# Both MLP products of a 1024-wide block as seven block products, in units of 1024 inner channels

## The reference

```python
h = rms_norm(x, g_mlp[l])
f = jnp.square(jax.nn.relu(jnp.einsum("bsd,df->bsf", h, w_1[l])))   # 1024 -> 4096 inner channels
x = x + jnp.einsum("bsf,fd->bsd", f, w_2[l])                        # 4096 -> 1024
```

## Time and profile before

| what | value |
|---|---|
| median of 3 runs | 2386.34 us (2386.21 to 2386.46) |
| the profiled execution | 2386.64 us |
| its span | 2384.8 us |
| PE, DVE, ACT, POOL busy | 2369.0, 1549.4, 902.7, 84.4 us |
| granted TensorE clock, mean | 0.998 |
| moved by DMA | 138.43 MB, 58 GB/s |

### The profile page before, as it was taken

How to read it: one execution, slowest core, us unless ns; L and a number is a source line. 1 busy time by engine, 2 the same in 40 slices (tenths; PEclk the granted TensorE clock), 3 DMA queues, 4 the chain that set the end, 5 groups by cost and what they waited for, 6 DMA issues and landing times.

```text
span 2384.8 us, 26302 instructions
## 1 busy us (share of the span) xinstructions
PE 2369.0 (99%) x10688; PEld 1923.4 (81%) x10688; DVE 1549.4 (65%) x2162; ACT 902.7 (38%) x1370; POOL 84.4 (4%) x103
## 2 busy tenths in 40 slices
PE   9999999999999999999999999999999999999998
PEld 7778688687788888888888888888888877888887
DVE  8899599598779744466655665534667544462377
ACT  6552442443512632333433343332343232222364
POOL 0000000000000000011111111000000000000000
PEclk9999999999999999999999999999999999999999
DMA  4201112012031112312212211112211111211222
GB/s 139 58 23 54 62 36 76 27 45 76 29 104 45 45 45 72 96 49 62 58 32 62 62 47 42 58 45 73 81 45 48 45 45 45 52 51 49 71 87 82
DMA packets 228321, 138.43 MB, mean 58 GB/s; under 512 B 15968, under 2 KB 219104, under 8 KB 228200
## 3 DMA queue, kind: packets, MB, share of 16 engines
q1 hardware_dynamic: 228200, 136.75, 19.5%
HBM read 127.78 MB, written 8.95 MB: 57 GB/s over the span
## 4 chain that ended last, share of the span: by engine, by line
PE 87%; DVE 8%; ACT 4%; issue 1%; DMA 0%; SPq 0%; DVEq 0%; ACTq 0%
PE bank L669 27%; PE bank L671 26%; PE bank L670 26%; PE bank L782 3%; DVE q_all L2872 1%; DVE v L2028 1%; PE bank L1055 1%; ACT whi L1193 1%; DVE uw L2638 0%; PE bank L1037 0%; PE bank L971 0%; DVE uc L2280 0%; DVE wlo L1899 0%; ACT un_hi L1209 0%; ACT bank L1419 0%
## 5 line engine op out<-in xcount | busy, mean ns | idle before, releaser
L669 PE MATMUL bank<-h_hi,whi 128*128 128x512 f32 x1984 | 780.2, 393 | 1.5 <-DVE h_lo L1921 1.1
L671 PE MATMUL bank<-h_hi,wlo 128*128 128x512 f32 x1984 | 773.0, 390 | 0.0
L670 PE MATMUL bank<-h_lo,whi 128*128 128x512 f32 x1984 | 772.6, 389 | 0.0
L669 PEld LDWEIGHTS bank<-h_hi,whi 128*128 128x128 f32 x1984 | 372.6, 188 | 83.0 <-DVE h_lo L1921 2.2
L670 PEld LDWEIGHTS bank<-h_lo,whi 128*128 128x128 f32 x1984 | 372.7, 188 | 79.5 <-issue 2.9
L671 PEld LDWEIGHTS bank<-h_hi,wlo 128*128 128x128 f32 x1984 | 372.7, 188 | 78.0
L1899 DVE TENSOR_TENSOR wlo<-raw,whi 128x1024 fp32r<-128x1024 f32 (+2 forms) x233 | 272.4, 1172 | 141.2 <-ACT whi L1193 139.6
L1193 ACT ACTIVATE whi<-raw 128x1024 fp32r<-128x1024 f32 (+2 forms) x233 | 232.5, 1004 | 269.0 <-PE bank L671 220.2
L2373 DVE SCALAR_TENSOR_TENSOR tmp<-bank,factor 128x512 f32<-128x512 f32 x64 | 44.2, 690 | 89.8 <-PE bank L671 89.8
L782 PE MATMUL bank<-v,gate_w 128*128 128x512 f32 x224 | 97.4, 592 | 0.0
L2392 DVE TENSOR_TENSOR x<-x,bank 128x512 f32<-128x512 f32 x96 | 65.7, 685 | 47.3 <-ACT bank L1500 46.4
(11 more groups left out here) (406 smaller groups left out, 3675.3 us busy)
## 6 DMA issues: line engine op xcount, KB each, us to landing
raw<-in_w_in SPq DMA_DIRECT2D x90, 512.0 KB, 3.7
raw<-in_w SPq DMA_DIRECT2D x40, 512.0 KB, 3.9
raw<-in_w_b_out SPq DMA_DIRECT2D x16, 384.0 KB, 3.1
raw<-in_w SPq DMA_DIRECT2D x24, 256.0 KB, 2.7
raw<-in_w SPq DMA_DIRECT2D x48, 128.0 KB, 2.2
raw<-in_w_out SPq DMA_DIRECT2D x11, 512.0 KB, 3.4
raw<-in_w_a_out SPq DMA_DIRECT2D x8, 512.0 KB, 3.8
raw<-in_w_o SPq DMA_DIRECT2D x8, 512.0 KB, 3.9
```

The source lines that it names most:

```text
L669: pe.matmul(target, lh, rh, start=start, stop=False, skip_group_check=True)
L670: pe.matmul(target, lh, rl, start=False, stop=False, skip_group_check=True)
L671: last = pe.matmul(target, ll, rh, start=False, stop=stop and point is not None, skip_group_check=True)
```

## The change

`PIECES`, `TURNS` and the plain first product go. The MLP becomes 28 **units** (`UNITS`), each of seven products. A unit covers two output tiles and 1024 input channels: four tiles are the first half of the blocks (a11, a12) and four the second (a21, a22). A product of a unit has 4 tiles x 3 = 12 matmuls. Units 0 to 15 (`UP`) are the first product, units 16 to 27 the second product of the first 3072 inner channels, in three sets of four (`DOWN`). Output tiles of the first product are u//4 * 8 + u % 4 and that plus 4.

- **Steps.** `ORDER` lists PE's steps, one product each: 1 and 5 of unit w, 7 of w-1, 2 of w, 3 of w-1, 6 of w, 4 of w-1. The PSUM scheme is the one of before.
- **Granules.** The left factor of each product is 128x512, a granule. ACT makes the high part (`ghi`), DVE the low part (`glo`), 4 or 5 steps ahead (`LEAD`); there are six rooms.
- **Weights.** SP loads two blocks of 128x1024 a unit, in two sets of buffers; `raw` is one of them. POOL forms the sums in place, as 128x512, four per unit.
- **Right sides.** Seven combinations of four tiles each (`c_hi`, `c_lo`) are kept. The first set is made from x in and after the output product, by scaled joins (L2510). For the sets of the second product they come from DRAM: b11 to t4 of units 0 to 11 are stored to `ff_dram`, 128x512 at a time, and loaded back in place of the set in use, four tiles of a name when its last product is done (`load_piece`, L635), and split 2 and 3 steps later (`pieces_at`).
- **Activation.** The results of a unit are emptied by DVE (`relu`, `relu_both`), squared by ACT, and their differences made by DVE (`three_differences`, `last_difference`).
- **The factor** is made from 8 one-column matmuls (`x1_stat`) and spread by 8 transposes.
- **The last 1024 inner channels** are units 12 to 15 of the first product; they are stored, and loaded as `ff_in` for the plain second product, whose first two column blocks PE computes together, tile by tile (`tiles_together`).

```diff
-PIECE = 4
-PIECES = 6
-TURNS = (0, 2, 1, 3)
+UP = D_FF // (2 * P)
+DOWN = FC - 1
+UNITS = UP + 4 * DOWN
+ORDER = [(w - late, n) for w in range(UNITS + 1) for n, late in ((1, 0), (5, 0), (7, 1), (2, 0), (3, 1), (6, 0), (4, 1))
+         if 0 <= w - late < UNITS]
+GRANULES = 6
+LEAD = (5, 5, 4, 4, 4, 5, 5)
...
+            def load_unit(u, *parts):
+                rows, row0, *columns = unit_columns(u)
+                for m in parts:
...
+                        for n in ((6, 3), (7, 4))[m]:
+                            w.wait_ge(*at("g", u - 2, n))
+                    sp.dma_start(unit_raw[u % 2][m][:].rearrange("p (k c) -> p k c", k=DT), tiles_of(rows, row0, DT, columns[m], P)).then_inc(
+                        *landed(f"unit{u % 2}_{m}", ("unit_in", u, m)))
...
+            for u in range(UNITS):
+                if 2 <= u + 1 < UNITS:
+                    load_unit(u + 1, 0)
+                store_ff(u - 2, "b21", "t4")
+                if u >= 2:
+                    load_piece(u - 2, "t4")
+                if 2 <= u + 1 < UNITS:
+                    load_unit(u + 1, 1)
+                load_piece(u, "b11")
+                load_piece(u, "t1")
...
+                store_ff(u - 1, "b22")
...
+                store_ff(u - 1, "b12", "t1", "t3", "t2")
+                load_piece(u, "t2")
...
-            def product(e, c, n):
+            def product(u, n):
...
+                room, name = granule_room(TURN[u, n]), RIGHT[n]
+                w.wait_ge(*at("g", u, n))
+                for p in range(HK):
+                    cs = slice(p * P, (p + 1) * P)
+                    w.wait_ge(*at("c_lo", unit_set(u), name, p))
+                    three_products(b[:], (ghi[room][:, cs], glo[room][:, cs]), (c_hi[name][p][:], c_lo[name][p][:]), n in (1, 5) and not p,
+                                   [("unit", u, n)] if p == HK - 1 else None)
...
+            for u, n in ORDER:
+                product(u, n)
+                if (u, n) == (0, 2):
+                    x1_stat()
+                if (u, n) == (0, 7):
+                    for half in range(2):
+                        w.wait_ge(*at("x1_r"))
+                        spread(0, half, "x1_factor", sum_banks[half])
...
-            for j in range(DT):
-                block(("w1", FC - 1, j, "end"), h2, "h2")
-            for j in range(DT - 2):
+            for half in range(2):
+                tiles_together([("w2", FC - 1, j) for j in range(2)], half, ff, f"ff{FC - 1}", order=FF_TILES)
+            for j in range(2, DT - 2):
...
+            for k, (u, n) in enumerate(ORDER):
+                granules(k + lead(k))
+                if n == 1:
+                    last_difference(u - 2)
...
+                if n == 6:
+                    three_differences(u - 1)
+                    third_seed(u)
...
+                new_combos(u, n)
...
+                pool.tensor_tensor(total[:], a21, a22, ALU.add).then_inc(*up("pool_done", ("sum", u, 5)))
+                w.wait_ge(*at("unit_in", u, 0))
+                pool.tensor_tensor(a21, a11, a21, ALU.subtract).then_inc(*up("pool_done", ("sum", u, 7)))
+                w.wait_ge(*at("g", u, 1))
+                w.wait_ge(*at("sum", u, 7))
+                pool.tensor_tensor(a11, total[:], a11, ALU.subtract).then_inc(*up("pool_done", ("sum", u, 6)))
+                w.wait_ge(*at("g", u, 2))
+                w.wait_ge(*at("sum", u, 6))
+                pool.tensor_tensor(a12, a12, a11, ALU.subtract).then_inc(*up("pool_done", ("sum", u, 3)))
```

More of the change, by code:

```diff
@@ L387, in build_program @@
[L387 to L391, removed]
+        ff_in = sb("ff_in", "h", 0, [P, DT, 2 * SEQ])
@@ L690, in hold @@
                 return banks[i]
-            def product(e, c, n):
-                kind, room, right = PRODUCTS[n]
-                k = number[kind, e, c]
+            def product(u, n):
                 if n == 1:
-                    b = hold(4 * (c % 2), "chain", e, c)
-                    hold(1, "first", e, c)
-                    w.wait_ge(*at("free", *earlier["chain", e, c]))
+                    b = hold(4 * (u % 2), "chain", u)
+                    hold(1, "first", u)
+                    w.wait_ge(*at("free", *earlier["chain", u]))
@@ L1542, in scalar, with first_seed @@
-            for j in range(DT):
-                ahead(number["w1", FC - 1, j, "end"] + 2)
-                for half in range(2):
-                    t = tmp[half]
-                    w.wait_ge(*at("relu", FC - 1, j, "end", half))
-                    act.activation(t[:], t[:], ACT.Square).then_inc(*did(("relu_square", FC - 1, j, "end", half)))
-                    w.wait_ge(*now("act_done"))
-                    w.wait_ge(*at("m", PIECES - 1, 3, 4))
-                    split_hi(("ff_hi", j, half), ff[0][j][:, cut(half)], t[:])
+            def first_seed(u):
+                w.wait_ge(*at("unit", u, 1))
+                w.wait_ge(*at("free", *earlier["first", u]))
+                act.activation(bank("first", u)[:], bank("chain", u)[:], ACT.Copy).then_inc(*did(("first_seed", u)))
@@ new lines, in fifth_copy, with fourth_seed @@
+            def fifth_copy(u):
+                w.wait_ge(*at("unit", u, 5))
+                if u >= 2:
+                    w.wait_ge(*at("fifth_used", u - 2))
+                act.activation(fifth[u % 2][:], bank("fifth", u)[:], ACT.Copy).then_inc(*did(("fifth_copy", u), ("free", "fifth", u)))
+            def fourth_seed(u):
+                w.wait_ge(*at("unit", u, 7))
+                w.wait_ge(*at("free", *earlier["fourth", u]))
+                act.activation(bank("fourth", u)[:], bank("chain", u)[:], ACT.Copy).then_inc(*did(("fourth_seed", u)))
@@ L1551, in scalar @@
+            for n in range(1, 4):
+                ff_part(n, 0)
+            for n in range(1, 4):
+                ff_part(n, 1)
             for j in range(DT - 2):
@@ new lines, in last_difference, with third_seed @@
+            def last_difference(u):
+                if not 0 <= u < WHOLE:
+                    return
+                w.wait_ge(*at("ff", u, "b21"))
+                w.wait_ge(*at("ff", u, "t2"))
+                difference(u, "t4", tmp[tmp_of(u, "b21")], tmp[tmp_of(u, "t2")])
+            def third_seed(u):
+                w.wait_ge(*at("unit", u, 6))
+                w.wait_ge(*at("fifth_copy", u))
+                w.wait_ge(*at("free", *earlier["third", u]))
+                dve.tensor_tensor(bank("third", u)[:], bank("chain", u)[:], fifth[u % 2][:], ALU.add).then_inc(*did(("third_seed", u)))
```

788 lines of the change are left out of this document (467 added, 321 removed).

## The result

The changed kernel takes 2352.61 us (2351.89 to 2353.5, 4 runs) where the kernel before takes 2386.4 (2386.21 to 2387.25): a ratio of 0.9858, 95% interval 0.9841 to 0.9875. The forecast was 2346.0, range 2341 to 2363. Faster was right, but by 33.8 us (1.4%), and the time is 6.6 us above the forecast. The seven-block products gave what was forecast; some 135 us behind them PE loses 8.4 us.

What follows compares the result with a forecast made beforehand. TensorE's matmul count times pitch was taken as the bound: 2386.3 - 43.5 + 0.9 = 2343.7 us, plus 1 (start), 0.5 (end) and 0.5 (set changes) gives 2345.7, forecast as 2346 us, range 2341 to 2363.

Steps and rivals of the forecast that it cites:

- 192 matmuls and the narrow ones: TensorE: 192 fewer matmuls at 0.2267 us save 43.5 us; one-column sums and small transposes, less the old sums, add 0.9.
- The start: From the output product's last matmul into unit 0: VectorE's joins and low parts nearly in time; 1 us of TensorE waiting.
- The set changes: Three changes of right sides: VectorE near 95% busy, 3 to 4 us behind at worst, without stopping TensorE; 0.5 us taken.
- the end: Start of the last plain second product: its tiles land and are split about when TensorE wants them; 0.5 us taken.
- GpSimd's addition: Four 128x512 additions per unit, taken at 1.48 us each, 5.9 us a unit, bounds 0.74 to 3.4 us each.
- The sharing: GpSimd's additions slow VectorE instructions reading two SBUF tensors: 0.45 us per us of GpSimd's work, 2.7 us a unit.
- by its numbers the exclusion is about half: Reading of the earlier trace: GpSimd and VectorE exclude each other from SBUF only about half, not fully.
- The transfers: Unit and set loads and stores fit, 303 GB/s at set changes against 366; loads land in 4 to 7 us.
- the rest is whether the others keep up with a unit: Beyond 2343.7 us, time depends on other engines keeping pace with TensorE's 84 matmuls, 19.04 us, per unit.
- The circle of transfers: Rival, 0.08: store, VectorE, ScalarE and GpSimd waits set each unit's pace, up to 2428 us; 6 us of room found.
- VectorE late: Rival, 0.13: full SBUF exclusion and 0.69 us pitch make TensorE stop at set changes and start; 2354 to 2368 us.
- the forecast's own 2343.7 to 2352: Likeliest case, 0.77: the matmul saving arrives, with TensorE waits of 0 to 8 us together.

Runs made afterwards that it cites:

- experiment 4: Experiment 1 with three of GpSimd's four additions per unit made over 8 columns instead of 512: 2340.91 us, ratio 0.9812 to the kernel before.
- experiment 1: The changed kernel with the ring of PSUM banks restored to place 4 behind the seven-block products: 2343.57 us, ratio 0.9822 to the kernel before.
- Experiments 8: Experiment 1 with the fourth of four matmuls of each tile group in every unit product left out: 2313.57 us, ratio 0.9692 to the kernel before.
- 9: Experiment 1 with a quarter of the unit products' matmuls left out and three of four GpSimd additions over 8 columns: 2273.77 us, ratio 0.9528.

## Why the prediction was right, and where not

- **192 matmuls and the narrow ones** (-43.5 + 0.9): right. Less 1 us for the start and 0.5 for the set changes the MLP should have given 41.1 us; it gave 41.9. There is some luck in the 41.9: the start cost 1.4 us more than taken, and against that stand some 1.5 us that the kernel before lost over the pitch in its pieces, behind the first 45 us, where the changed kernel loses none. No term counted these.
- **The start** (1 us): too small. PE lost 2.4 us there, and did not with narrow additions (experiment 4); I had put GpSimd at 1 us of DVE's 23 in all. Only the 0.5 us at the first seed is followed back to DVE's joins beside additions. Where PE waited was also wrong: for the first seed behind ACT and for the factor's column (L866, 0.4 us), not for the b22 pieces.
- **The set changes** (0.5) **and the end** (0.5): nothing was lost at either. DVE's busy share at the first change was 33.8 of 43 us, below the 95% I named.
- **GpSimd's addition**: 1.29 to 1.30 us alone against 1.48 taken. The sharing (0.45 us of DVE per us of GpSimd) was about right on average: by experiment 4 it is 38 us for 94, 0.41. But "by its numbers the exclusion is about half" misread the rows. Instruction by instruction it is whole: in experiment 1, between 990 and 1600 us, 70 DVE instructions without a PSUM bank begin with more than 0.15 us of an addition to go, and 69 of them end 0.55 us after it. The earlier trace rows has it too: the 128x1024 one ends at 1159.56, 1.08 us after the addition that ends at 1158.48. The average is lower because much of an addition has no such instruction beside it. And it falls on the same instructions in each unit:

```profile
L3209 POOL TENSOR_TENSOR first_sum<-unit_raw x14: 1285/1300/2188, 995.8 to 1518.3; 128x512 f32<-128x512 f32 x14
...
L2498 DVE TENSOR_TENSOR glo<-raw,ghi x84: 673/685/1821, 1037.3 to 1557.7; 128x512 fp32r<-128x512 f32 x84
L2498 DVE TENSOR_TENSOR glo<-first_sum,ghi x28: 677/1104/1717, 1014.8 to 1535.9; 128x512 fp32r<-128x512 f32 x28
```

- **The transfers**: right. The unit's loads landed in 4.1 us, those of the set in 5.3 to 5.4, the stores in 2.1:

```profile
ff_dram<-tmp SPq DMA_DIRECT2D x100, 256.0 KB, 2.1
...
unit_raw<-in_w SPq DMA_DIRECT2D x28, 512.0 KB, 4.1
c_in_t<-ff_dram SPq DMA_DIRECT2D x24, 512.0 KB, 5.4
```

- **The step that failed** is "the rest is whether the others keep up with a unit". It put all new waits in the MLP. The change also moved the ring's place, and with it the banks of everything behind; the wait of 5.6 us and the half clock behind it, 8.4 us by the table, were in no term. That the time still fell into the range is luck: its upper part was meant for VectorE late in the MLP, and a wait that no term spoke of filled it. A bank's owner and its next writer could have been read from the program, by counting the places that the removed blocks took.
- **The circle of transfers** (rival, 0.08) did not set the pace, so the chance was on the right side. But its 6 us of room was wrong: 0.8 us (19.04 less 18.27) is what the units of the first product have. I followed the load to PE's need of the granule and found time enough. I left out what is queued behind the granule on ACT and DVE: while these wait for the sum, the seeds behind it wait too, and PE needs those first. The forecast was right in its time here with a margin that it did not know.
- **VectorE late** (rival, 0.13): its 2354 to 2368 lies just above the result, as the forecast's own 2343.7 to 2352 lies just below it, but the mechanism did not occur; in the MLP PE's waits after the first 45 us are zero.

The Trainium skill, "GPSIMD Engine Reference", section Specifications, says that GpSimd and VectorE contend for their shared interfaces when VectorE reads two operands in SBUF. Experiments 8 and 9 bear it out with 1.1 us for 0.69 and 1.75 for 0.69. In the units of the changed kernel this cost nothing, at its start up to 2.4 us (experiment 4): what it costs depends on whether PE, or a circle longer than PE's work, waits for the lengthened instruction.

## What to carry to other kernels

When a change removes or adds users of a ring of buffers, count the places modulo the ring up to the end of the program: a stage that was not touched can get a bank whose reader is late, and one line puts it back. The room of a circle isn't measured by the busy share of the engines in it, nor by the due time of the datum that comes late alone: what stands in line behind the wait on each in-order engine may be due first. A cheap way to measure it is to take work from the engine that bounds the time, or to add some to a suspect, and to see from which point the time no longer follows.

## What the runs showed of the hardware

Behind a wait of PE of 5.6 us the granted clock was 0.50 over 6.8 us in both kernels, and around one of 11.0 us it was 0.50 over 13.6 us. That is the lower of the two levels, 1.2 GHz; it added 2.7 us to the 5.7 of the first wait. A GpSimd addition of 128x512 takes 1.29 us, less than twice the 0.74 of 128x256 in the earlier trace rows, and one DVE difference of 128x512 beside it takes 1.75 to 1.78 us for 0.69: it loses 1.1 us to one addition, ending 0.55 us after it, while instructions that read a bank kept their 0.7 us beside additions. Why the 3.4 us at half clock behind the gates' first matmuls is missing in experiment 1 stays open; of the twelve traces seven have it and five, all with the ring at 4, do not.
